# Triangular inverse of the chunked RWKV scan: 16x16 diagonal blocks on GpSimd, two levels on TensorE, groups interleaved

## The reference

```
sa = einsum('bhvk,bhk->bhv', s, kk_t)
s = s * w_t - sa (kk_t * a_t) + v_t k_t ;  y_t = s r_t
```

## Time and profile before

| | us |
|---|---|
| median of 3 runs | 2637.7 (2627.84 to 2640.29) |
| the profiled execution | 2621.45 |
| its span | 2619.8 |
| PE busy | 2062.3 (79%) |
| DVE busy | 1571.4 (60%) |
| POOL busy | 1192.6 (46%) |
| ACT busy | 657.9 (25%) |
| mean granted clock of TensorE | 0.943 |

### The profile page before, as it was taken

How to read it: one execution, slowest core, us unless ns; L and a number is a source line. 1 busy time by engine, 2 the same in 40 slices (tenths; PEclk the granted TensorE clock), 3 DMA queues, 4 the chain that set the end, 5 groups by cost and what they waited for, 6 DMA issues and landing times.

```text
span 2619.8 us, 28860 instructions
## 1 busy us (share of the span) xinstructions
PE 2062.3 (79%) x7970; PEld 1167.3 (45%) x7970; DVE 1571.4 (60%) x3823; ACT 657.9 (25%) x1481; POOL 1192.6 (46%) x1143
## 2 busy tenths in 40 slices
PE   7988989998998979877788676666766666667767
PEld 3544358898898856533344222222222222222222
DVE  1288636775876774755555566665655656655562
ACT  3244202223232243221122212112221122222222
POOL 4000000000000000776666777777777777777775
PEclk9998999999999989998889899999899998999899
DMA  6143331312322152998998999999999999999997
GB/s 202 55 139 111 124 113 49 113 49 66 97 65 63 51 185 65 361 345 333 332 337 327 352 368 353 345 365 371 336 366 344 351 372 350 361 374 349 348 368 277
DMA packets 266256, 650.62 MB, mean 248 GB/s; under 512 B 21280, under 2 KB 120192, under 8 KB 265856
## 3 DMA queue, kind: packets, MB, share of 16 engines
q0 software_dynamic: 150336, 552.67, 56.6%
q1 hardware_dynamic: 115776, 96.28, 12.2%
HBM read 631.04 MB, written 17.83 MB: 248 GB/s over the span
## 4 chain that ended last, share of the span: by engine, by line
PE 39%; issue 17%; DMA 15%; DVE 13%; another core or an unknown queue 6%; POOL 5%; ACT 3%; SPq 1%; DVEq 0%; POOLq 0%; ACTq 0%; PEldq 0%
PE bank L1367 15%; DMA arena<-in_peer_v_dram,arena 11%; POOL arena L1076 5%; PE bank L1847 5%; PE bank L789 3%; DMA arena<-in_peer_u_dram,arena 3%; PE bank L771 3%; PE bank L975 2%; DVE arena L1349 1%; PE bank L775 1%; PE bank L745 1%; PE bank L792 1%; PE bank L798 1%; PE bank L706 1%
## 5 line engine op out<-in xcount | busy, mean ns | idle before, releaser
L1367 PE MATMUL bank<-arena 128*128 128x512 f32 x2048 | 1024.8, 639 | 381.2 <-DMA arena<-in_peer_v_dram,arena 201.5
L1349 DVE CUSTOM_DVE_ANT_0 arena<-arena 128x1024 f32<-128x1024 f32 x512 | 623.2, 1224 | 397.4 <-DMA arena<-in_peer_u_dram,arena 353.9
L1367 PEld LDWEIGHTS bank<-arena 128*128 128x128 f32 x2048 | 382.5, 200 | 1018.5 <-issue 851.6
L1076 POOL DMA_INDIRECT arena<-in_peer_v_dram,arena x512 | 604.4, 1180 | 241.5 <-issue 127.6
L1076 POOL DMA_INDIRECT arena<-in_peer_u_dram,arena x512 | 541.8, 1058 | 177.9 <-issue 142.7
L1109 ACT ACTIVATE arena<-arena 128x128 f32<-128x128 f32 x512 | 195.3, 399 | 917.6 <-PE bank L1367 499.1
L837 POOL MEMSET arena<- 128x4096 f32 x1 | 3.5, 3516 | 585.4 <-DVE arena L618 585.4
L1847 PE MATMUL bank<-arena 128*128 128x512 f32 x432 | 206.6, 609 | 10.0 <-PEq L384 6.2
L771 PE MATMUL bank<-arena 128*128 128x128 f32 x960 | 118.6, 276 | 15.9 <-DVE arena L649 15.9
L1847 PEld LDWEIGHTS bank<-arena 128*128 128x128 f32 x432 | 84.1, 196 | 83.0 <-issue 72.9
L771 PEld LDWEIGHTS bank<-arena 128*128 128x128 f32 x960 | 112.2, 191 | 19.2 <-issue 14.2
(11 more groups left out here) (290 smaller groups left out, 2422.2 us busy)
## 6 DMA issues: line engine op xcount, KB each, us to landing
arena<-in_w_mod_dram SPq DMA_DIRECT2D x24, 1024.0 KB, 6.2
arena<-in_peer_wq_dram SPq DMA_DIRECT2D x32, 512.0 KB, 7.4
arena<-in_w_in_dram SPq DMA_DIRECT2D x27, 512.0 KB, 4.1
arena<-kr_scratch SPq DMA_DIRECT2D x96, 128.0 KB, 3.5
arena<-in_peer_u_dram,arena POOLq DMA_INDIRECT x512
arena<-in_peer_v_dram,arena POOLq DMA_INDIRECT x512
bk_scratch<-arena POOLq DMA_DIRECT2D x8, 768.0 KB, 3.6
kr_scratch<-arena POOLq DMA_DIRECT2D x8, 768.0 KB, 5.4
```

The source lines that it names most:

```text
L1076: pool.indirect_dma_start(ring[:, j % RING, :], None, table, bass.IndirectOffsetOnAxis(ap=idx[:, hi % 4, j:j + 1].bitcast(U32), axis=0)).t ...
L1349: nc.vector.tensor_tensor_reduce(u_ring[:, j % RING, :], u_ring[:, j % RING, :], h2cur, 1.0, 0.0, ALU.mult, ALU.add, acts[:, h % 2, j:j + ...
L1367: m = nc.tensor.matmul(PO[h][:, :], diag[:, j % 4], v_ring[:, j % RING, 512 * h:512 * h + 512], start=hp == 0 and j == 0, stop=hp == HEADS ...
```

## The change

Of the inverse only the last two levels stay on TensorE (from 16x16 to 64x64). The 16x16 diagonal blocks, 4 for each of 2 heads, 4 chunks and 2 directions, 64 in all, are inverted by substitution on GpSimd, one block on each of 64 partitions. To get them there, SP writes NBD of direction 0 and MBD of direction 1 to DRAM (tri_scratch, four DMAs), reads the diagonal blocks back with one partition for each block, and after the 30 GpSimd instructions writes the inverses and their transposes out (inv_scratch) and reads them back as rows of 16 numbers on 128 partitions. VectorE spreads them with a mask (own_block) into ZZ and XX.

The program of a block is cut into a front (loads, turning, key-values, masks, triangle's transpose) and a back (levels, QQ). The front of block n+1 now runs within the step of block n, ahead of its back; BKT and MBD have two buffers for it. The loop over pairs is written out, with no Fori. GpSimd inverts block n+1 while the back of block n runs. In stage 1 the semaphores of the weight blocks and latents are shared by two loads each, and their waits are for both. Fewer level masks are made.

```diff
+SUB = 16
+TRI = DH // SUB * (SUB * DH + SUB)
...
+    def steps4(front, do, tail):
+
+        front(0, 0)
+        for n in range(NBLK):
+            p, b = n // 3, n % 3
+            nxt = ((n + 1) // 3, (n + 1) % 3) if n + 1 < NBLK else None
+            chain = ((n - 1) // 3, (n - 1) % 3) if n else None
+            do(p, b, nxt, chain)
         tail()
...
+        def triangles_out(p, b):
+            n = 3 * p + b
+            for d in range(2):
+                if d == 0:
+                    sp.wait_ge(front_vector[0], NFV * n + FV["go"])
+                else:
+                    sp.wait_ge(front_scalar[1], NFS * n + FS["m"])
+                tri = [NBD, MBDs[n % 2]][d]
+                dst = tri_dram.rearrange("(d i h e) -> d h i e", d=2, h=2, e=TRI)[d][:, :, 0:DH * DH].rearrange("h i (r c) -> h r i c", c=DH)
+                sp.dma_start(dst[0], tri[LOW, d, :, 0:DH]).then_inc(triangles_saved, 16)
+                sp.dma_start(dst[1], tri[HIGH, d, :, DH:P]).then_inc(triangles_saved, 16)
+
+        def triangles_in(p, b):
+            n = 3 * p + b
+            sp.wait_ge(triangles_saved, 64 * n + 64)
+            src = tri_dram.rearrange("(s e) -> s e", e=SUB * DH + SUB)[:, 0:SUB * DH].rearrange("s (r c) -> s r c", c=DH)
+            sp.dma_start(sub[0:8 * 2 * NB], src[:, :, 0:SUB]).then_inc(triangles_loaded, 16)
+
+        def inverses_out(p, b):
+            n = 3 * p + b
+            if n:
+                sp.wait_ge(base_loaded, 16 * n)
+            sp.wait_ge(base_steps, SUB_STEPS * n + SUB_STEPS)
+            sp.dma_start(inv_dram.rearrange("w s e -> s w e"),
+                         sub_inv[0:8 * 2 * NB].rearrange("s w i j -> s w (i j)")).then_inc(inverses_saved, 16)
+
+        def inverses_in(p, b):
+            n = 3 * p + b
+            sp.wait_ge(inverses_saved, 16 * n + 16)
+            if n:
+                for d in range(2):
+                    sp.wait_ge(back_vector[d], NBV * (n - 1) + BV["x"])
+            src = inv_dram.rearrange("w (n b) (r c) -> (b r) (w n) c", b=8, c=SUB)
+            sp.dma_start(base_rows, src).then_inc(base_loaded, 16)
+
+        def row_load(p, j):
+            if p or j:
+                sp.wait_ge(modulation_rows, 4 * p + j)
+            at = p * D + 2 * D + 256 * j
+            sp.dma_start(wmr, wmod_v[:, :, at:at + 256]).then_inc(wmod_row_weights, 16)
+
+        def front(p, b):
+            front_loads(p, b)
+            read_loads(p, b)
+            row_load(0, 0)
+            front_loads(0, 1)
+            triangles_out(p, b)
+            triangles_in(p, b)
+            read_loads(0, 1)
+
+        def do(p, b, nxt, chain):
+            n = 3 * p + b
+            if n:
+                row_load(p, b)
+            inverses_out(p, b)
+            inverses_in(p, b)
+            if nxt:
+                triangles_out(*nxt)
+                triangles_in(*nxt)
+            if b == 2:
+                row_load(p, 3)
+            if n + 2 < NBLK:
+                front_loads((n + 2) // 3, (n + 2) % 3)
+            if n + 2 < NBLK:
+                read_loads((n + 2) // 3, (n + 2) % 3)
+        steps4(front, do, lambda: None)
...
+        S = slice(0, 8 * 2 * NB)
+        inv, tri = sub_inv[S, 0], sub[S]
+
+        def base_inverse(p, b):
+
+            n = 3 * p + b
+            k = [0]
+
+            def step(i):
+                k[0] += 1
+                i.then_inc(base_steps, 1)
+                pool.wait_ge(base_steps, SUB_STEPS * n + k[0])
+
+            pool.wait_ge(triangles_loaded, 16 * n + 16)
+            if n:
+                pool.wait_ge(inverses_saved, 16 * n)
+            step(nc.gpsimd.tensor_tensor(inv, tri, sub_ident[S], ALU.add))
+            for j in range(SUB - 2, 0, -1):
+                w = SUB - 1 - j
+                t = sub_tmp[S, 0:j * w].rearrange("p (a b) -> p a b", b=w)
+                step(nc.gpsimd.tensor_tensor(t, tri[:, 0:j, j:j + 1].broadcast_to([8 * 2 * NB, j, w]),
+                                             inv[:, j:j + 1, j + 1:SUB].broadcast_to([8 * 2 * NB, j, w]), ALU.mult))
+                step(nc.gpsimd.tensor_tensor(inv[:, 0:j, j + 1:SUB], inv[:, 0:j, j + 1:SUB], t, ALU.add))
+            step(nc.gpsimd.tensor_copy(sub_inv[S, 1].rearrange("p i j -> p j i"), inv))
...
+        def base(n, dst, w, name):
+
+            for d in range(2):
+                at = 2 * NB * (d if w == 0 else 1 - d) + NB * d
+                src = base_rows[:, at:at + NB].unsqueeze(2).broadcast_to([P, NB, P // SUB, SUB])
+                own = own_block.rearrange("p (a b) -> p a b", b=SUB).unsqueeze(1).broadcast_to([P, NB, P // SUB, SUB])
+                nc.vector.tensor_tensor(dst[:, d].rearrange("p i (a b) -> p i a b", b=SUB), src, own, ALU.mult).then_inc(back_vector[d], 1)
+
+        def front(p, b):
+            dve.wait_ge(n_zeroed, 2)
+            dve.wait_ge(masks_made, n_masks)
+            even_products(p, b)
+            masked_odd(p, b)
+
+        def do(p, b, nxt, chain):
+            n = 3 * p + b
+            if chain:
+                split(*chain, 0)
+            if nxt:
+                even_products(*nxt)
+            if chain:
+                advance(*chain, 0)
+            if nxt:
+                masked_odd(*nxt)
+            dve.wait_ge(base_loaded, 16 * n + 16)
+            base(n, ZZ, 0, "z")
+            if chain:
+                split(*chain, 1)
+            if n:
                 for d in range(2):
+                    dve.wait_ge(back_products[d], NBP * (n - 1) + BP["q"])
+            base(n, XX, 1, "x")
+            for d in range(2):
+                dve.wait_ge(back_products[d], NBP * n + BP["a0"])
+                nc.vector.tensor_tensor(AA[:, d], v3(W1[d][:, :]), bcast(lvl[:, d, 0], ALL, ALL), ALU.mult).then_inc(back_vector[d], 1)
+            if chain:
+                advance(*chain, 1)
+            for d in range(2):
+                dve.wait_ge(back_products[d], NBP * n + BP["z0"])
+                nc.vector.tensor_tensor(ZZ[:, d], v3(W2[d][:, :]), ZZ[:, d], ALU.add).then_inc(back_vector[d], 1)
+            if chain:
+                split(*chain, 2)
+            for d in range(2):
+                dve.wait_ge(back_products[d], NBP * n + BP["a1"])
+                nc.vector.tensor_tensor(AA[:, d], v3(W1[d][:, :]), bcast(lvl[:, d, 1], ALL, ALL), ALU.mult).then_inc(back_vector[d], 1)
+            if chain:
+                advance(*chain, 2)
+            for d in range(2):
+                dve.wait_ge(back_products[d], NBP * n + BP["x1"])
+                nc.vector.tensor_tensor(XX[:, d], v3(W1[d][:, :]), XX[:, d], ALU.add).then_inc(back_vector[d], 1)
+            if chain:
+                split(*chain, 3)
+                advance(*chain, 3)
+                if chain[1] == 2:
+                    total(chain[0])
...
+        def do(p, b, nxt, chain):
+            n = 3 * p + b
+            MBD, BKT = MBDs[n % 2], BKTs[n % 2]
+            if nxt:
+                turn_inputs(*nxt)
+            if chain:
+                read_state(*chain, 0)
+            if nxt:
+                key_values(*nxt)
+            if chain:
+                apply_chunk(*chain, 0)
+            if nxt:
+                odd_products(*nxt)
+            mod_row(p, b)
+            if nxt:
+                turn_triangles(*nxt)
+            if chain:
+                pe.wait_ge(modulation_rows_moved, 4 * p + b + 1)
+                read_state(*chain, 1)
+            for d in range(2):
+                pe.wait_ge(back_vector[d], NBV * n + BV["z"])
+                pe.wait_ge(front_scalar[d], NFS * n + FS["m"])
+                if nxt:
+                    pe.wait_ge(front_vector[d], NFV * (n + 1) + FV["go"])
+                four(lambda i: nc.tensor.matmul(W1[d][:, P * i:P * i + P], MBD[:, d, i], ZZ[:, d, i],
+                                                start=True, stop=True), back_products[d])
+            if chain:
+                apply_chunk(*chain, 1)
+            for d in range(2):
+                pe.wait_ge(back_vector[d], NBV * n + BV["a0"])
+                if nxt:
+                    pe.wait_ge(front_scalar[d], NFS * (n + 1) + FS["m"])
+                four(lambda i: nc.tensor.matmul(W2[d][:, P * i:P * i + P], XX[:, d, i], AA[:, d, i],
+                                                start=True, stop=True), back_products[d])
+            if chain:
+                read_state(*chain, 2)
+            for d in range(2):
+                pe.wait_ge(back_vector[d], NBV * n + BV["z0"])
+                four(lambda i: nc.tensor.matmul(W1[d][:, P * i:P * i + P], MBD[:, d, i], ZZ[:, d, i],
+                                                start=True, stop=True), back_products[d])
+            for d in range(2):
+                four(lambda i: nc.tensor.transpose(W2[d][:, P * i:P * i + P], ZZ[:, d, i], ident), back_products[d])
+            if chain:
+                apply_chunk(*chain, 2)
+            if b == 2:
+                mod_row(p, 3)
+            for d in range(2):
+                pe.wait_ge(back_vector[d], NBV * n + BV["a1"])
```

(66 more changed lines are left out.)

332 lines of the change are left out of this document (151 added, 181 removed).

## The result

| | before | after |
|---|---|---|
| median of the runs, us | 2632.8 (4 runs, 2625.5 to 2640.3) | 2454.3 (4 runs, 2441.5 to 2462.1) |
| profiled execution, us | 2621.45 | 2452.15 |
| span, us | 2619.8 | 2450.5 |
| first load of stage 4 | 357.8 | 359.6 |
| end of the last head sum | 947.5 | 767.6 |

The ratio is 0.9317 (0.9266 to 0.9369). 2454 us was measured where 2480 was forecast. Stage 4 is 181.7 us shorter where the working had 162. Start of the stage +1.8, stage -181.7, behind it +10.6, together the -169.3 of the two profiled executions. The 10.6 lie in stages that the change doesn't touch, with the same instructions; the runs of one kernel spread over 15 to 21 us here, and the medians differ by 178.5.

A forecast was written before the change was run, and what follows sets the result against it. TensorE was taken to bound stage 4, VectorE close behind. Twelve blocks at a 32 us period cut 590 us to 428; 2621.45 - 162 + 4 = 2463.5, plus 16.2 gives 2480 us, range 2440 to 2560.

The forecast's parts named there:

- TensorE's levels: Stage 4's inverse: three levels with transposes leave TensorE, 13.5 us a block less, 27.8 us left.
- VectorE next to it: Stage 4: 16 fewer 512-column operations take 11.0 of VectorE's 37.5 us a block, 26.5 left, as long as TensorE.
- The order of one block: Stage 4's period drawn from rows: 28.5 us, 32.0 with a second row, 30.5 with a head sum; 30.9 with 0.6 added.
- The detour: Small inverses through DRAM and GpSimd: 27 us, ends 16 and 42, hidden under a block with 2.3 us to spare.
- the 1.1 us that I put on each period: Stage 4: added to 30.9 us for nearness to the edge and the inverse's transfer queued behind row weights, giving T = 32.
- The second row: Stage 4: 0.6 us a block on top, since its weights are loaded behind the triangle's two transfers.
- The ends of the stage: Stage 4: 49.7 us to the first level, eleven periods 352, then 10.5 and 15.7: 428 against 590, 162 us gained.
- Stage 1: Weight blocks waited for in pairs delay the last product: bounds 0 and 5.3 us, 4.0 us taken as lost.
- From the profiled execution to the median: Whole kernel: the median lay 16.2 us above the profiled execution; carried over, 2463.5 becomes 2480 us.
- A: Rival in stage 4: the detour at its upper ends, 42 us, is late; T = 37.3, 2553 us; chance 0.20 with what lies between.
- B: Rival in stage 4: GpSimd instructions cost more, SP's ring decides; break-even 1.19 us each, 2740 us at 1.4; chance 0.08.
- C: Rival in stage 4: gaps drop TensorE's clock to 1.2 GHz for a third of its work; T = 41, 2579 us; chance 0.07.

The follow-up runs named there:

- b_two_levels: Kernel before with three of five inverse levels left out, old order, no detour, loop kept: stage 4 460.7 us, ratio 0.9516 to the kernel before.
- a_row_early: Changed kernel with a pair's second row weights loaded ahead of the triangle's two transfers: stage 4 400.1 us, ratio 0.9250 to the kernel before.
- a_pool_20: Changed kernel with 20 more GpSimd instructions of 56 elements a block: stage 4 423.6 us, ratio 0.9361 to the kernel before.
- a_no_detour: Changed kernel without the detour, small inverses a constant set once on GpSimd: stage 4 384.7 us, ratio 0.9270 to the kernel before.
- a_pool_56: Changed kernel with 56 more GpSimd instructions of 56 elements a block: stage 4 562.8 us, ratio 0.9918 to the kernel before.
- a_serial: Changed kernel with the next block's front behind this block's back on every engine, detour kept: stage 4 660.9 us, ratio 1.0270 to the kernel before.

## Why the prediction was right

**TensorE's levels: right.** 13.5 us a block were to go, and 27.8 to stay. In nine steady blocks (433.8 to 710.6 us) PE is busy 259.1 us, 28.8 a block, where ten blocks of the kernel before (427.9 to 901.9 us) have 42.9 each: 14.1 less. b_two_levels gave 129 us of the stage with nothing but the levels gone.

**VectorE next to it: right in kind, 2.5 us too high.** 26.5 us a block were left by the sum; in the same nine blocks it is busy 216.0 us, 24.0 a block. The window that I started from held a head sum of 3.7, which comes once in three blocks. This changed nothing, as the order of the block was drawn from single rows.

**The order of one block: right, term by term.** 28.5, 32.0 and 30.5 forecast; 28.0, 31.5 and 30.0 measured once the second row's weights are there (a_row_early). The mean of the changed kernel over nine blocks is 30.8, where 30.9 stood; that it is so near is luck, since the order was 0.5 too long and the late row 0.3 too cheap.

**The detour: hidden, and it was not as near to the edge as I made it.** The term that was mis-sized is the 1.1 us that I put on each period, "the mean being this near to the edge". Over eleven periods that is 12 of the 20 us by which the stage came out shorter. Detour and spare time came out at 23.8 and 2.8 us, where 27 and 2.3 stood, and a_pool_20 shows that 7.3 us more in it leave nine steady blocks as long as they were. The terms under it were off both ways. The gather of 2048 pieces of 64 B took 3.0 us where 6.4 was computed from rows of 512 B and more, the gather of 1024 took 2.9 for 4.1; GpSimd took 10.7 for 9.9; the 128 pieces of the inverses took up to 6.1 for 2.2, behind the 1 MB of row weights. The chosen form of price for GpSimd was near: 0.21 to 0.29 us and 0.08 to the next, where the 64-column select had given 0.23 and 0.06. From 14 to 56 elements the time rises by 0.08 us, 1.9 ns an element, and about two thirds of the longest are a fixed part. The rule from the Trainium skill, "GPSIMD Engine Reference", section 3.1 (two-input operations at about 2.6 cycles an element), is near to that: an estimated 2.2 ns at the 1.2 GHz that the section reckons with.

The prediction named the spreads and the chain's decay as instructions that could block GpSimd. No spread ran beside a GpSimd instruction of the detour, so the spreads' 0.69 us show nothing of it. The decay (L723, two SBUF inputs) did in 28 of its 88 instructions. Its rows in the changed kernel, and in a_no_detour (ns min/median/max):

```profile
L723 DVE SCALAR_TENSOR_TENSOR arena<-arena x88: 331/345/476, 419.7 to 759.2; 128x128 f32<-128x128 f32 x88
...
L719 DVE SCALAR_TENSOR_TENSOR arena<-arena x88: 340/344/360, 410.0 to 736.8; 128x128 f32<-128x128 f32 x88
```

The 28 take 0.369 us on average and up to 0.476, the other 60 take 0.349 at most; a GpSimd instruction of 14 elements takes up to 0.317 us beside a decay and 0.223 at most without one. In kind this agrees with the Trainium skill, "SBUF — State Buffer", section "Who interferes with whom", by which a VectorE instruction with two SBUF inputs contends with a GpSimd one that reads SBUF. The price is some 0.1 us where it happens and under 1 us over the stage on each side, where up to 5 us a block were feared; nine blocks took 268.6 us with the detour (a_row_early) and without.

**The second row: mis-sized.** 0.6 us a block were put on top for it; the third block of a pair lost 1.9 to 4.1, so 0.9 a block, as a_row_early shows. The cause is the one named, the load behind the triangle's transfers. In the first of the three the lower clock behind the gap made it larger: there the row took 5.4 us, in the other two 3.7.

**The ends of the stage.** The first level came 43.7 us after the first load where 49.7 was worked out, since the gathers landed sooner. The eleven periods took 328.7 us, where 352 less the 3 for the last block stood. From the last block's first level to the end it was 35.6 us where 29.2 stood (13.5 and 15.7): the last block has a second row (3.5), which was left out, and the granted clock was 0.74 from 740 to 768 us. The last period was 25 us, so more than the 3 us were saved there. Together -6.0, -20.3 and +6.4: the 20 us.

**Stage 1.** 4.0 us lost were forecast. TensorE's timeline of the changed kernel answers to the earlier trace rows:

```profile
39.28 8.78 PE L2021 MATMUL bank<-arena 128*2 128x256 f32 x32 [4.66 <-DMA arena<-in_w_mod_dram]
47.99 0.24 PE L2025 MATMUL bank<-arena 24*128 24x24 f32 x1
```

32 records wait for the last load instead of 16 and take 8.8 us instead of 5.3: 3.4 us later by the next instruction (44.6 before, 48.0 now). Of these 1.8 are left at the start of stage 4 in these two profiles, and about 3 over all profiles (above). So the mechanism holds, and the 4.0 us were somewhat too many.

**From the profiled execution to the median.** 2454 against 2480 is about 26 us. The stage gave 20 of them and its start 2, and the stages behind it took 11 back, which nothing in the change explains. The other 14 are the 16.2 us that were carried over because the profiled execution before was a fast one; for the changed kernel the median lies 2.2 us above it. So the nearness of the total says less than the stage does.

**The rivals.** A (a late detour) needed terms at their upper ends that were not there. B (GpSimd at over 1.19 us an instruction) is out with 0.21 to 0.29 us; a_pool_56 shows that its place was right, the ring on SP. Its formula with the 31.3 us that GpSimd takes there gives 42.0 us for the 42.4 measured: the triangle's issues that it lacked and the gathers that it had too dear nearly cancel. C (the clock): 0.99 over the steady blocks, 0.94 in the window with the late row.

## What to carry to other kernels

When an engine is the bound by busy time, first draw one period of the new order with durations from rows; that gave each of the three periods to 0.5 us here, and the margin for "near the edge" was the largest error. A detour through DRAM of 24 us can cost nothing in steady blocks, if a whole block of other work stands between its start and its use; the same detour without that look-ahead lost to the original. Look at what else is issued in the same queue behind its waits: here one load of weights, not the detour, took all that was lost in steady blocks. And the spare time of such a detour is not a fixed number: with 7.3 us more in it, its transfers no longer queued behind that load.

## What the runs showed of the hardware that was not expected

2048 pieces of 64 B into 128 partitions landed 3.0 us after the issue (3.0 to 3.3 in twelve), 1024 pieces of 64 B into 64 partitions in 2.9 (2.7 to 4.6), against 6.2 for 1024 pieces of 1 KB: small pieces were far cheaper than a price for each piece made them.

The same kernel before took 2491 us in one session and 2644 in another. For the changed kernel stage 4 was nearly as long (402.7 against 408.0), and the difference lay behind it: 1535 against 1683 us, with 369 against 336 GB/s moved. It is not simply the chip: the runs name it by number, and the kernel before took 2629 us on number 12 beside a_serial and 2479 us on number 12 beside a_pool_20. The cause is open.
